# Reordering the work between the expert router and the first expert stage of a fused decoder step

## The reference

```python
h = h + cross_attn(rmsnorm(h, norm_xattn), k, v, w_xq, w_xo)
hn = rmsnorm(h, norm_moe)
logits = hn @ w_router + b_router                  # 264 tokens x 32 experts
top_v, top_i = lax.top_k(logits, 4)                # 4 experts for each token
gates = jax.nn.softmax(top_v)
# tokens sorted by expert; for each expert e:
gu = xb @ w_gate_up[e] + b_gate_up[e]              # 1024 -> 2048
glu = clip(up) + 1, gate * sigmoid(1.702 * gate)
y = (glu product) @ w_down[e] + b_down[e]          # 1024 -> 1024
out[token] += gate_weight * y
```

## Time and profile before

| what | value |
|---|---|
| median of three runs | 1410.22 us |
| span of the profiled execution, first to last instruction | 1407.9 us |
| mean granted clock of TensorE | 0.998 |
| TensorE busy | 1376.7 us, 98% of the span |
| ScalarE, VectorE, GpSimd busy | 217.9, 441.5, 27.9 us |
| bytes moved, mean rate | 497.25 MB, 353 GB/s |
| chain that ended last, by what it went through | TensorE 83%, DMA 14%, VectorE 2% |

### The profile page before, as it was taken

How to read it: one execution, slowest core, us unless ns; L and a number is a source line. 1 busy time by engine, 2 the same in 40 slices (tenths; PEclk the granted TensorE clock), 3 DMA queues, 4 the chain that set the end, 5 groups by cost and what they waited for, 6 DMA issues and landing times.

```text
span 1407.9 us, 16140 instructions
## 1 busy us (share of the span) xinstructions
PE 1376.7 (98%) x6438; PEld 673.5 (48%) x6438; DVE 441.5 (31%) x902; ACT 217.9 (15%) x403; POOL 27.9 (2%) x48
## 2 busy tenths in 40 slices
PE   9999999999999999999999999999999999999997
PEld 7788887677757633333333333333333332332322
DVE  5634345871461312221211312212113121121213
ACT  2220022052123411110101111011011010110102
POOL 0000002200000000000000000000000000000000
PEclk9999999999999999999999999999999999999999
DMA  7644446975379799999999999999999999999995
GB/s 256 210 154 154 175 142 200 376 268 190 118 283 398 284 413 428 429 425 430 427 430 427 430 427 429 428 429 429 428 428 429 430 427 430 427 430 426 431 426 228
DMA packets 71575, 497.25 MB, mean 353 GB/s; under 512 B 8752, under 2 KB 10216, under 8 KB 46824
## 3 DMA queue, kind: packets, MB, share of 16 engines
q1 hardware_dynamic: 65180, 477.94, 82.5%
q0 software_dynamic: 4432, 15.53, 3.0%
q10 hardware_dynamic: 1924, 3.23, 0.7%
HBM read 488.61 MB, written 8.24 MB: 353 GB/s over the span
## 4 chain that ended last, share of the span: by engine, by line
PE 83%; DMA 14%; DVE 2%; issue 1%; ACT 0%; SPq 0%; DVEq 0%
PE bank L1492 78%; DMA ring<-in_w_gate_up 8%; DMA flat<-in_w_gate_up 6%; PE bank L1503 4%; DVE wide L1418 1%; DMA flat<-in_x_prompt 0%; DVE wide L1475 0%; ACT wide L618 0%; PE bank L1946 0%; ACT L628 0%; ACT L658 0%; ACT wide L609 0%; SPq L506 0%; DVE wide L1466 0%; DVE wide L1395 0%
## 5 line engine op out<-in xcount | busy, mean ns | idle before, releaser
L1492 PE MATMUL bank<-ring,wide 128*64 128x512 f32 (+2 forms) x1696 | 405.5, 595 | 6.9 <-DMA ring<-in_w_gate_up 6.0
L1492 PE MATMUL bank<-wide 128*64 128x512 f32 (+6 forms) x1024 | 283.3, 574 | 8.7 <-DVE wide L1418 6.3
L1492 PE MATMUL bank<-tokT,ring 128*128 128x264 f32 x1152 | 266.0, 389 | 0.8 <-DVE tokT L959 0.8
L1492 PEld LDWEIGHTS bank<-ring,wide 128*64 128x64 f32 (+2 forms) x1696 | 132.4, 140 | 259.9 <-issue 246.1
L1492 PEld LDWEIGHTS bank<-tokT,ring 128*128 128x128 f32 x1152 | 217.8, 191 | 42.4 <-issue 6.4
L1492 PEld LDWEIGHTS bank<-wide 128*64 128x64 f32 (+4 forms) x1024 | 94.6, 152 | 171.9 <-issue 121.9
L609 ACT ACTIVATE wide<-bank 64x512 f32<-64x512 f32 (+3 forms) x104 | 58.2, 560 | 348.3 <-PE bank L1492 227.0
L1442 DVE TENSOR_SCALAR wide<-bank 128x512 f32<-128x512 f32 x32 | 22.1, 692 | 274.3 <-PE bank L1492 274.3
L1492 PE MATMUL bank<-flat,wide 128*64 128x512 f32 (+2 forms) x408 | 92.3, 589 | 3.7 <-DMA flat<-in_w_gate_up 3.7
L1492 PE MATMUL bank<-conv,wide 128*64 128x512 f32 (+1 forms) x400 | 91.1, 596 | 0.3 <-ACT wide L609 0.3
L890 ACT ACTIVATE wide<-wide 128x512 f32<-128x512 f32 x32 | 20.2, 630 | 428.6 <-DVE wide L1442 428.6
(11 more groups left out here) (257 smaller groups left out, 735.1 us busy)
## 6 DMA issues: line engine op xcount, KB each, us to landing
ring<-in_w_gate_up SPq DMA_DIRECT2D x64, 2048.0 KB, 26.1
ring<-in_w_down SPq DMA_DIRECT2D x32, 2048.0 KB, 28.1
flat<-in_w_gate_up SPq DMA_DIRECT2D x16, 2048.0 KB, 26.9
conv<-in_w_gate_up SPq DMA_DIRECT2D x16, 2048.0 KB, 25.5
wide<-in_w_gate_up SPq DMA_DIRECT2D x16, 2048.0 KB, 25.7
tokT<-in_w_gate_up SPq DMA_DIRECT2D x16, 2048.0 KB, 27.0
ring<-in_w_in SPq DMA_DIRECT2D x15, 2048.0 KB, 12.3
wide<-in_w_down SPq DMA_DIRECT2D x8, 2048.0 KB, 25.2
```

The lines of the kernel that those rows point to most:

```text
L1492: last[0] = pe.matmul(out, lhsT, rhs, start=start, stop=stop)
```

## The change

Seven edits between the last projection and the end of the first pair:

1. `sum_tokens` is split. `sum_early` (the blocks summed so far) runs before the second last `route`, `sum_last` (the last block) right after it and ahead of the last `route`. The one-column products became three-column ones with a table `units`, into one bank. The transposes of block 6 go behind the last `route`.
2. All six `cache_rows` go from before the mask into the first pair: two behind stage 2, four behind stage 3. Their ScalarE copies move with them.
3. `hidden_bias` of the first pair goes ahead of the mask; `stay_warm(2)` there becomes `stay_warm(4)`, and the three behind the ranks become one. Its one-hot operand is made earlier, in another piece of SBUF.
4. The total count gets a bank and a semaphore step of its own, so that VectorE starts on the ranks without it; the count of passes is worked out after the gathered tokens, and `value_load` goes behind the first pair on all four engines.
5. `gather`, `copy_rows`, `turn_rows` of the first pair are replaced by `gather_turned`: the tokens are the stationary operand and the selection moves, so that the result has the channel in the partition at once. Each block of 128 channels takes three products of 128 columns. Eight blocks in three pieces: 2 and 2 ahead of stage 1, 4 ahead of stage 2. ScalarE scales the tokens in five pieces rather than three.
6. SyncE issues chunks 3 and 8 right after chunk 0 (behind the samples' attention, `so` 3) and not after the last projection and the sums; their places move (`first_acts`, `onehot`, `gT`, `sqo`).
7. In the stream of ScalarE the wait for `v_out` goes ahead of the squares; on VectorE the subtraction for the softmax goes behind the selection.

The core of the diff:

```diff
@@ PLAN
-PLAN += [("xo", 5, D_, (0, 1)), ("xtok", 3, A_, (3, 4, 5)), ("xo", 3, D_, (1, 0)), ("mrow", 1, A_, (0,)),
-         ("rt", 3, D_, (2, 6, 7)), ("rs", 1, A_, (1,)), ("xtok", 3, A_, (3, 4, 5)), ("mrow", 3, A_, (1, 6, 7)),
-         ("srow", 2, A_, (0, 3)), ("rank", 1, D_, (2,))]
+PLAN += [("xo", 5, D_, (0, 1)), ("xtok", 3, A_, (3, 4, 5)), ("xo", 3, D_, (1, 0)),
+         ("rs", 1, A_, (0,)), ("rt", 3, D_, (2, 6, 7)), ("xtok", 3, A_, (3, 4, 5)), ("rank", 1, D_, (6,)),
+         ("total", 1, D_, (7,)), ("mrow", 4, A_, (4, 5)), ("srow", 2, A_, (4, 5))]
@@ sync
-            for j, name, k in ((2, "so", 1), (4, "so", 1), (5, "so", 3), (0, "so", 3), (1, "xo", 3), (3, "xo", 7)):
+            for j, name, k in ((2, "so", 1), (4, "so", 1), (5, "so", 3), (0, "so", 3), (6, "so", 3), (8, "so", 3), (1, "xo", 3), (3, "xo", 7)):
                 filled(sp, name, k)
                 first_chunk(FIRST_SLOT.index(j))
-            first_chunk(3)
-            filled(sp, "rs")
-            first_chunk(8)
             filled(sp, "xtok", 5)
             first_chunk(7)
-            sp.wait_ge(S["passes_ready"], 1)
-            n = sp.value_load(npass[0:1, 0:1], min_val=0, max_val=MAXP - 1)
...
@@ scalar
+            s.wait_ge(S["v_out"], 16)
             for k in range(KB):
...
-            move("mrow", 0, mrows[0][:, 0:512], 512, 11)
             b = filled(s, "rs")
...
-            for t, n in TILES_P:
-                copy(xtok[0:n, t, :], acc[0:n, t, :], rr[0:n, t:t + 1]).then_inc(S["xtok_ready"], 1)
-            for k in range(1, 4):
+            for h in range(2):
+                for t, n in TILES_P:
+                    cols = slice(512 * h, 512 * h + 512)
+                    copy(xtok[0:n, t, cols], acc[0:n, t, cols], rr[0:n, t:t + 1]).then_inc(S["xtok_ready"], 1)
+            s.wait_ge(S["lg_ready"], 1)
+            s.activation(gts, gts, ACT.Exp).then_inc(S["lg_exp"], 1)
+            for k in range(4):
...
@@ vector
+            for q in range(2):
+                v.wait_ge(S["xg_gathered"], q + 1)
+                v.tensor_tensor(out=xg[:, 2 * q:2 * q + 2, :],
+                                in0=bank[4 + q][:, 0:256].rearrange("p (k n) -> p k n", k=2),
+                                in1=bc(gains[:, 2 * q:2 * q + 2], P), op=ALU.mult).then_inc(S["xg_quarter"], 1)
+            v.wait_ge(S["xgt_turned"], 2)
+            v.tensor_tensor(out=xg[:, 4:8, :], in0=bank[6][:, :].rearrange("p (k n) -> p k n", k=4),
+                            in1=bc(gains[:, 4:8], P), op=ALU.mult).then_inc(S["xg_ready"], 2)
...
@@ tensor
+            def gather_turned(h, b, blocks):
+
+                for n, i in enumerate(blocks):
+                    out = b[:, n * P:n * P + P]
+                    for t in (0, 1):
+                        rows = xtok[:, t, 512 * h:512 * h + 512].rearrange("p (s d m) -> p s m d", d=P, m=2)
+                        mm(out, rows[:, i // 2, i % 2, :], selT[:, t, :], t == 0, False)
+                    rows = slice(32 * h, 32 * h + TS)
+                    ends = xtok[rows, 2, 0:512].rearrange("p (s d m) -> p s m d", d=P, m=2)
+                    mm(out, ends[:, i // 2, i % 2, :], selT[rows, 2, :], False, True)
+
+            for name, k in (("xo", 6), ("rs", 0), ("rt", 0), ("xtok", 3)):
+                emptied(pe, name, k)
...
+            hidden_bias(first_pair, 0)
+            emptied(pe, "xtok", 4)
+            stay_warm(4)
+            pe.wait_ge(S["mask_ready"], 1)
...
+            stay_warm(1)
+            pe.wait_ge(S["sel_ready"], 1)
+            pe.wait_ge(S["xtok_ready"], 3)
+            gather_turned(0, bank[4], (0, 1))
+            last[0].then_inc(S["xg_gathered"], 1)
...
+                if first:
+                    emptied(pe, "xtok", 5)
+                    gather_turned(0, bank[5], (2, 3))
+                    last[0].then_inc(S["xg_gathered"], 1)
+                    pe.wait_ge(S["xg_quarter"], 1)
+                    gate_up(0, 0)
+                    emptied(pe, "rank")
+                    pe.wait_ge(S["xtok_ready"], 5)
+                    gather_turned(1, bank[6], range(4))
+                    last[0].then_inc(S["xgt_turned"], 2)
+                    pe.wait_ge(S["xg_quarter"], 2)
+                    gate_up(0, 1)
+                    pe.wait_ge(S["raw_kept"], 1)
+                    cache_rows("mrow", 0, kept_x, 11)
+                    cache_rows("mrow", 1, kept_x, 11)
...
             experts(first_pair, 0, 0, first=True)
+            pe.wait_ge(S["passes_ready"], 1)
+            n = pe.value_load(npass[0:1, 0:1], min_val=0, max_val=MAXP - 1)
```

143 lines of the change are left out of this document (73 added, 70 removed).

## The result

The changed kernel takes 1418.45 us (median of 4 runs, 1415.92 to 1423.97) against 1410.36 (4 runs, 1409.88 to 1412.86) beside it: ratio 1.0061, 95% interval 1.0036 to 1.0086. The forecast was 1410.2 with a range up to 1413.2. Measured a second time, it took 1415.51 (7 runs, 1413.16 to 1422.61), ratio 1.0042 (1.0018 to 1.0066). The profiled execution has a span of 1419.0 against 1407.9, 11.1 more. Two executions far off all others, one of experiment 4 (1598.45 us) and one of the kernel before (7561.48 us), are left out of the medians and ratios.

A forecast was written before the change was run, and what follows sets the result against it. The DMA weight stream was taken to bound the end, hanging on stage 9: stage 1 6.1 us earlier, 6.1 going back before stage 9, sum 0, time 1410.2 us. Own range 1408.8 to 1412.0; 8 in 10, 1407.0 to 1413.2.

The forecast's parts named there:

- the even traffic: Weight stream before the change: 425 to 431 GB/s without a break from the fifteenth slice to the last but one.
- The end follows stage 9: Chunk 16, issued when stage 9 is done, sets the end of the weight stream; stage 1 does not.
- chunks 3 and 8 early: SyncE's earlier issue of these chunks goes into idle DMA time; worth 0.
- chunk 28: Next place the stream could break, behind stage 21; 1.9 us of slack, no gap expected near 583.
- the stream hangs on stage 1: Faster rival: first refill sets the end, all 6.1 us come through, 1404.1; with in-between cases 0.17 for over 2.8 us.
- Sums, mask, warm products, ranks: Last projection to gather: warm products, not the mask, set the ranks' start at 474.1; gather starts at 476.75, against 478.41.
- The new gather: Ahead of stage 1: 0.1175 us a record, 12 products 2.82 us; stage 1 starts at 479.6, 6.1 us earlier.
- the 0.15 that the prediction itself named as a sign of being wrong: Gather on TensorE: a record of over 0.15 us would show the prediction wrong.
- what goes back: Between stage 1 and stage 9: 2.82 gather, 2.96 cache rows, 0.3 waiting, 6.1 us in sum.
- load-bound at 0.191: Slower rival: strided weights make 48 gather records 0.191 us each, 3.5 us more, 1413.7; chance 0.12.
- loads and products overlap: TensorE, read from the earlier trace: a record of 128 columns with its own load takes 0.1175 us.
- The clock: TensorE from last projection to chunk 16: the prediction had no term for a falling clock and took durations from the trace.

The follow-up runs named there:

- experiment 4: Kernel before with one transpose instead of four in each of the six cache row groups: 1414.57 us, ratio 1.0031.
- (5): The changed kernel measured again without an edit: 1415.51 us, ratio 1.0042.
- (3): Changed kernel with every second gather block taking its 8-row product first, so row counts change less often: 1413.85 us, ratio 1.0027.
- (9): Changed kernel with the gather's 8-row products left out, so the last 8 tokens are not gathered: 1410.01 us, ratio 0.9993.
- (2): Changed kernel with two warm products in TensorE's standstill and three more between last projection and sums: 1416.29 us, ratio 1.0038.
- (6): Changed kernel with two warm products in TensorE's standstill and the gather's 8-row products alternated in order: 1414.33 us, ratio 1.0018.
- (7): Changed kernel with the standstill filled by two warm products and chunks 3 and 8 issued where the kernel before issues them: 1414.73 us, ratio 1.0032.
- (13): Changed kernel with standstill filled and gather rows alternated, narrow products, measured again on another chip: 1413.64 us, ratio 1.0017.
- (1): Changed kernel with two warm products in the 0.78 us in which TensorE waits for ScalarE: 1414.87 us, ratio 1.0026.
- (10): Changed kernel, standstill filled, gather rows alternated, sums, router, ranks and total widened to 126 or 128 columns: 1415.47 us, ratio 1.0026.
- (12): Changed kernel, standstill filled, gather rows alternated, sums, ranks and total widened to 126 or 128 columns, router at 32: 1413.48 us, ratio 1.0019.

## Why the prediction was wrong, step by step

(The prediction lets the even traffic begin with the fifteenth slice; by the earlier trace rows that one has 413 GB/s and the sixteenth 428. Nothing hangs on it.)

*The end follows stage 9*: right, and all else rests on it. Chunk 16 to the end of the span is the same within 1.2 us in eighteen traces, chunks 3 and 8 early are worth nothing, no gap came at chunk 28, and the rival "the stream hangs on stage 1" is out: in (5) chunk 9 comes 4.6 us earlier than before, behind the same P, and the kernel is slower.

*Sums, mask, warm products, ranks*: right within 0.3 us when the clock holds. Ranks at P + 7.0 in (5) (forecast 6.8, bound by the warm products and not by the mask), gather at P + 9.47 (forecast 9.42).

*The new gather*: **this term failed first.** It was priced at 0.1175 a record, 2.82 for 24. It takes 4.35 ahead of stage 1 and 4.39 behind it, 0.182 a record, over the 0.15 that the prediction itself named as a sign of being wrong; 3.1 us for both. Stage 1 is 4.6 earlier and not 6.1, and what goes back is 8.1 and not 6.1: 4.39 for the gather, 3.30 for the cache rows with their wait (forecast 3.26), and 0.40 because the first three stages, with other work between them, take 3.58 us each and not the 3.45 that they took back to back (485.73 to 496.08 in the kernel before). The row it was priced by the earlier trace rows has products on 128 rows only, while a third of the new ones stand on 8 rows. Single records of the first profile start at 492.184, 492.301 (128 rows), 492.512, 492.734 (8 rows), 492.941, 493.161, 493.279 (128 rows). Each change has two long steps: 0.21 to the first record of the new row count and 0.22 from that to the second; from there on it is 0.118 again. Together that is 0.19 more than two steps of 0.118. A similar step stands where weights of 128 columns give way to weights of 8 columns on the same 128 rows: in the router's group 467.726 is followed by 467.931, 0.21, where its other records on 128-column weights come at 0.11. In the gather it is the change that costs and not the 8 rows: in (3), where two 8-row products stand side by side, their third and fourth record (485.761, 485.879) come at 0.118. Fourteen changes inside the pieces make 2.7 of the 3.1 us. The rival "load-bound at 0.191" had nearly the right size and time (1413.7; 1413.5 as estimated above), by the wrong mechanism and so by luck: (9) has the same strided weights and takes 0.13. Where the first long step comes from shows in the loads of (5), in three stretches that follow each other:

```profile
484.73 0.55 PEld L1505 LDWEIGHTS bank<-wide 128*128 128x128 f32 x4 [0.81 <-issue]
485.40 0.31 PEld L1505 LDWEIGHTS bank<-wide 8*128 8x128 f32 x2
485.83 0.55 PEld L1505 LDWEIGHTS bank<-wide 128*128 128x128 f32 x4
```

Four loads of 0.19 to 0.20 us each take 0.55 together, so on one row count they overlap. At both changes the next load begins 0.12 after the one ahead has ended (485.28 to 485.40, 485.71 to 485.83). The reason named in the expectation of (3), loads that wait for the running product, is near this, but not shown: the load at 485.40 begins 0.07 ahead of the modelled end of the record before it (485.47). Nor does a run show why the second long step, between records on the same rows, is there.

That loads and products overlap, as the prediction reads from the earlier trace rows, holds where the rows do not change: in (9) the 16 loads of the piece take 1.96 us, from 482.35, and its 16 records 2.08, from 482.36.

*The clock*: **this step was missing.** The forecast took TensorE's durations as given, because the clock stood at 1.00 in the profile of before. The change takes the cache rows, 24 transposes of 128 columns, from between the projection and the ranks, and puts bias and warm products there. In the first profile the clock fell behind P, which cost 7.6 us. It does not fall in every execution, and how much of the medians, 2 to 5 us above the estimate at full clock, is the clock's is not shown. The range had no room for it, although four warm products in the code said that the clock was in question there.

What brings the falls is settled in part. A standstill is not needed: the clock fell with TensorE busy throughout in (2), (6), (7) and (13), and held behind a standstill of 0.78 us in (3), (5) and (9). The products with 3 and 32 columns in sums, ranks and total are likely to have a part in it: none of the five profiles in which they are widened has a fall. They are not all of it, since taking transposes away from the kernel before was followed by one, with its products as they were (4), and since the changed kernel with all its narrow products ran without one in the profiles of (1), (3), (5) and (9). Which of the three groups counts, what the missing warm products and transposes do, and why one execution has a fall and the next has none, stays open.

*Sum.* 3.56 us at full clock, of which 3.1 are the gather, nearly all of it the row changes; 7.6 us of clock in the first profile, an unknown part of 2 to 5 us in the medians. Forecast: 0 and none.

## What to carry to other kernels

Price a product by a row with the same number of rows in the weights, and look at what stands on either side of it: products on few rows belong side by side (three changes fewer saved 0.57 us in (3)). When work is moved away from TensorE in front of a critical stretch, count the loss of its clock as a cost with its own range, even where the profile of before shows full clock there (in (4) and in the first profile of the changed kernel it fell to half, for 10.2 and 17.1 us); and measure twice before explaining one profile. A mean clock over the whole execution does not say where it fell (0.994 in (10) without a fall, 0.996 in (13) with one). And a threshold chosen after the runs is weaker evidence than one named ahead. What moves only the start of a stream is worth nothing as long as the stream runs dry later (chunk 9 came 4.6 us earlier in (5), and the kernel was 0.4% slower).

## What the runs showed of the hardware

- A change between weights of 128 rows and of 8 rows costs TensorE 0.19 us, in two long steps of 0.21 and 0.22 us among steps of 0.118 (first profile of the changed kernel). Four blocks of the gather take 4.38 us with 7 inner changes there, 3.81 with 4 in (3), and 2.08 with none in (9), the last with 16 records instead of 24.
- TensorE's clock can stand at half in one execution and at full in another of the same kernel on the same operands: 17.1 us at half clock between P and chunk 16 against none, 7.6 us of time. It can fall with TensorE busy throughout: 6.8 us at half clock from 477.5 in (6), 3.4 from 470.8 in (2).
- Eleven of the eighteen profiles also have 3.4 to 10.2 us at half clock in their first 21.2 us. Their P is at 466.8 to 468.8 (469.3 in (10), with its wider router products), that of the seven others at 466.8 to 467.3.
- Sums on 128 rows with 126 instead of 3 columns cost 0.3 us for a group of six records. In the first profile and in (12) single records on 128-column weights come 0.11 us apart with 3, 32 and 126 columns alike; what costs is mainly the records on 8-column weights (0.03 apart with 3 columns, 0.11 with 126). With sums, ranks and total so widened none of five profiles has a fall between P and c16, while four of four of their narrow partners have one; on the one chip that ran both, the medians do not differ (1410.30 and 1410.04; 1413.64 and 1413.65).
